# A two-layer hybrid decoder trunk on one core: the opening reads a transposed copy of x, and squares are summed on other engines

## The reference, cut to what matters

```python
def rmsnorm(x, gain):
    y = x * lax.rsqrt(jnp.mean(x * x, axis=-1, keepdims=True) + EPS)
    return y * gain
def swiglu(x, w_gate, w_up, w_down):
    return (jax.nn.silu(x @ w_gate) * (x @ w_up)) @ w_down
for l in range(DEPTH):                                  # 2
    x = x + 0.5 * swiglu(rmsnorm(x, ffn1_norm[l]), ...) # hidden width 2816
    x = x + token_mixing(rmsnorm(x, mix_norm[l]), ...)  # attentions A, B, C, gates, w_out
    x = x + 0.5 * swiglu(rmsnorm(x, ffn2_norm[l]), ...)
```

## Time and profile before

| | |
|---|---|
| median of three runs | 1139.65 us |
| profiled execution, its own time | 1140.59 us |
| its span, first to last instruction | 1138.8 us |
| PE busy | 1133.4 us (100%) |
| DVE busy | 770.4 us (68%) |
| ACT busy | 630.4 us (55%) |
| POOL busy | 70.3 us (6%) |
| chain that ended last | PE 98%, ACT 1%, DVE 1% |
| DMA, mean over the span | 182 GB/s; 326 and 318 GB/s in the first two of 40 slices |

### The profile page before, as it was taken

The page is one execution under the profiler, slowest core; times in us unless marked ns, Lnnn a source line. Parts: engine busy times, 40 slices in busy tenths (PEclk is TensorE's granted clock), DMA queues, the critical chain, the costliest instruction groups (busy, mean ns, idle before and its releaser), DMA issues.

```text
span 1138.8 us, 16092 instructions
## 1 busy us (share of the span) xinstructions
PE 1133.4 (100%) x5975; PEld 966.9 (85%) x5975; DVE 770.4 (68%) x1055; ACT 630.4 (55%) x941; POOL 70.3 (6%) x79
## 2 busy tenths in 40 slices
PE   9999999999999999999999999999999999999999
PEld 7888888888888888888888888888888888888887
DVE  5766666868768676655766856678676695766655
ACT  6644455666684564544564544466666745544542
POOL 3020000202000000000020200002110000000000
PEclk9999999999999999999999999999999999999999
DMA  9955554545544665556566555636445445655521
GB/s 326 318 175 196 187 196 134 185 144 190 148 148 150 220 222 189 190 178 219 173 166 228 185 185 186 204 98 216 148 156 178 176 156 186 222 185 201 194 87 37
DMA packets 138828, 207.34 MB, mean 182 GB/s; under 512 B 6898, under 2 KB 99876, under 8 KB 138756
## 3 DMA queue, kind: packets, MB, share of 16 engines
q1 hardware_dynamic: 137364, 205.02, 54.5%
q0 software_dynamic: 752, 0.79, 0.7%
q10 hardware_dynamic: 640, 0.55, 0.2%
HBM read 205.29 MB, written 1.05 MB: 181 GB/s over the span
## 4 chain that ended last, share of the span: by engine, by line
PE 98%; ACT 1%; DVE 1%; issue 0%; DVEq 0%; ACTq 0%; POOL 0%; POOLq 0%
PE bank L560 28%; PE bank L530 16%; PE bank L534 16%; PE bank L533 16%; PE bank L564 15%; PE bank L546 1%; PE bank L859 1%; PE bank L849 1%; PE bank L830 1%; ACT probs L1202 1%; PE bank L848 1%; PE bank L877 1%; PE bank L668 0%; PE bank L569 0%; ACT w_high L1016 0%
## 5 line engine op out<-in xcount | busy, mean ns | idle before, releaser
L1300 DVE TENSOR_TENSOR w_low<-raw,w_high 128x1024 fp32r<-128x1024 f32 x388 | 464.2, 1232 | 282.1 <-ACT w_high L1016 281.4
L1016 ACT ACTIVATE w_high<-raw 128x1024 fp32r<-128x1024 f32 x387 | 393.6, 1055 | 318.4 <-PE bank L564 173.5
L560 PE MATMUL bank<-xT,w_high 128*128 128x512 f32 x1388 | 331.6, 390 | 0.1
L560 PEld LDWEIGHTS bank<-xT,w_high 128*128 128x128 f32 x1388 | 257.0, 188 | 51.2 <-DVE xT L1318 0.2
L564 PEld LDWEIGHTS bank<-xT,w_low 128*128 128x128 f32 x1408 | 175.7, 191 | 3.6
L564 PE MATMUL bank<-xT,w_low 128*128 128x256 f32 x1408 | 178.6, 283 | 0.0
L530 PE MATMUL bank<-w_high,xT 128*128 128x512 f32 (+1 forms) x440 | 171.3, 389 | 0.0
L534 PE MATMUL bank<-w_low,xT 128*128 128x512 f32 (+1 forms) x440 | 168.1, 382 | 0.0
L533 PE MATMUL bank<-w_high,xT 128*128 128x512 f32 (+1 forms) x440 | 168.1, 382 | 0.0
L530 PE MATMUL bank<-w_high,oT_high 128*128 128x512 f32 x418 | 162.6, 389 | 0.0
L534 PE MATMUL bank<-w_low,oT_high 128*128 128x512 f32 x418 | 162.2, 388 | 0.0
(11 more groups left out here) (146 smaller groups left out, 770.8 us busy)
## 6 DMA issues: line engine op xcount, KB each, us to landing
raw<-in_w_in SPq DMA_DIRECT2D x92, 512.0 KB, 4.5
raw<-in_ffn_w_down SPq DMA_DIRECT2D x88, 512.0 KB, 4.2
raw<-in_ffn_w_gate SPq DMA_DIRECT2D x86, 512.0 KB, 4.0
raw<-in_ffn_w_up SPq DMA_DIRECT2D x86, 512.0 KB, 5.0
raw<-in_w_out SPq DMA_DIRECT2D x16, 512.0 KB, 4.4
raw<-in_w_branch_c SPq DMA_DIRECT2D x8, 512.0 KB, 3.9
raw<-in_w_branch_a SPq DMA_DIRECT2D x4, 512.0 KB, 4.0
raw<-in_w_branch_b SPq DMA_DIRECT2D x4, 512.0 KB, 5.9
```

What stands on the lines that cost most here:

```text
L560: return nc.tensor.matmul(bank[b0 + n][:, :], w_high[:, slot, column(k, n)], xT[:, k], start=k == 0, stop=full_last and k == KB - 1)
L1016: act.activation(w_high[:, slot], raw[:, in_slot, (p % 2) * 1024:(p % 2) * 1024 + 1024], ACT.Copy).then_inc(sem["high_ready"], 1)
L1300: dve.tensor_tensor(w_low[:, slot], raw[:, FILL_SLOT[p // 2], (p % 2) * 1024:(p % 2) * 1024 + 1024], w_high[:, slot].bitcast(F32), ALU.sub ...
```

## The change

1. The host gives the kernel a transposed copy of x (`x_turned`, 1024 by 256) and one array with all gains as columns. SP loads x_turned in five pieces (1, 1, 2, 2 and 2 blocks of 128 rows) into the space of `o_nat`, between the first weights; ACT's queue loads the gains. The first weights come by k block, and not by pair.
2. `cold_chunk` has no transposes. ACT and DVE make the high and low parts of xT from x_turned in SBUF (`cold_start`, `cold_pairs`). DVE rounds the first 512 columns of weights as well.
3. The squares are made by POOL: two multiplications and one addition of 1024 elements per partition, one addition of 512 and one of 256 (`sum_block_squares`). PE sums over the partitions with two matmuls of one column (`sum_squares`), ACT copies the result (`norm_sq`). The turn of the norm's row comes two groups of products later in PE's order than before, behind pair 4's narrow products.
4. The natural x is loaded later by POOL's queue, ahead of the rotary tables; the tables' own loads are issued after the second hidden tile. Gains need no transposes or copies.
5. TURNS_AT and CONTEXTS_AT of the first twin move from pairs 19 and 21 to 20 and 22, in both layers.

```diff
-TURNS_AT = (19, 27, 35, 42)
-CONTEXTS_AT = (21, 29, 37, 44)
+TURNS_AT = (20, 27, 35, 42)
+CONTEXTS_AT = (22, 29, 37, 44)
-WARM_FIRST, WARM_SECOND, WARM_THIRD = 6, 3, 6
+X_BLOCKS = ((0, 1), (1, 1), (2, 2), (4, 2), (6, 2))
+WARM = 11
...
+            load_x_turned(0)
+            load_x_turned(1)
+            first_rows(sp, 1, 1, half_landed[1], (1,))
+            load_x_turned(2)
+            first_rows(sp, 2, 2, fill_landed[FILL_SLOT[0]])
+            load_x_turned(3)
+            first_rows(sp, 4, 2, third_landed)
+            load_x_turned(4)
+            first_rows(sp, 6, 2, fill_landed[FILL_SLOT[1]])
...
+            def sum_block_squares():
+                for first, pieces in ((0, (0, 1, 2)), (D, (3, 4))):
+                    for piece in pieces:
+                        pool.wait_ge(x_turned_landed[piece], 16)
+                    v = x_turned[:, first:first + D]
+                    pool.tensor_tensor(x_squares[:, first:first + D], v, v, ALU.mult)
+                for width in (D, D // 2, D // 4):
+                    pool.drain()
+                    pool.tensor_tensor(x_squares[:, 0:width], x_squares[:, 0:width], x_squares[:, width:2 * width], ALU.add)
+                pool.drain().then_inc(block_squares_summed, 1)
...
+                pool.wait_ge(sem["hidden_ready"], value("hidden_ready", layer, 2))
...
+                if layer == 0:
+                    for half in range(HALVES):
+                        pool.dma_start(x[:, half], a["x"][0, half * P:half * P + P, :]).then_inc(x_loaded, 16)
...
-            def cold_row():
+            def sum_squares():
                 pe.wait_ge(sem["up_summed"], 1)
-                turn_row(0, 1, 4)
-                pe.wait_ge(rows_loaded, 16 * 3)
-                nc.tensor.transpose(bank[5][:, 0:GAIN_ROWS], gain_rows[0:GAIN_ROWS, :], ident[0:GAIN_ROWS, 0:GAIN_ROWS]).then_inc(gains_turned, 1)
+                pe.wait_ge(block_squares_summed, 1)
+                for half in range(HALVES):
+                    last = nc.tensor.matmul(bank[4][:, half:half + 1], x_squares[:, half * P:half * P + P], ones[:, 0:1].bitcast(F32),
+                                            start=True, stop=True)
...
+            def cold_pairs():
+                def block_low(kb):
+                    return dve.scalar_tensor_tensor(xT_low[:, kb, :], x_turned[:, kb * S:kb * S + S], gains_all[:, 0, G_FFN1 + kb:G_FFN1 + kb + 1],
+                                                    xT_high[:, kb, :].bitcast(F32), ALU.mult, ALU.subtract)
...
+                for p in range(1, 4):
+                    dve.wait_ge(sem["blocks_high"], p + 1)
+                    block_low(2 * p)
+                    block_low(2 * p + 1).then_inc(sem["blocks_low"], 1)
+                    low(0, p)
```

More of the change, by code:

```diff
@@ L114 @@
 }
[L117 removed]
+CREDIT = {"pair_used": RING, "low_ready": 2 * RING, "blocks_turned": -4}
 def ring_slots(items, mix_first, mix_items):
@@ L685, in cold_chunk @@
                     high_part(0, n, w_high, True)
+                pe.wait_ge(half_low, 1)
+                for n in range(4):
+                    high_part(0, n)
+                pe.wait_ge(block0_low, 1)
+                for n in range(4):
+                    low_part(0, n)
+                pe.wait_ge(sem["blocks_high"], 1)
                 pe.wait_ge(sem["high_ready"], value("high_ready", 0, 1))
@@ L688, in cold_chunk @@
                     high_part(1, n, w_high)
-                turn(1, 0, 1)
                 pe.wait_ge(sem["blocks_low"], 1)
-                for k in range(2):
-                    for n in range(4):
-                        low_part(k, n)
+                for n in range(4):
+                    low_part(1, n)
                 pe.wait_ge(sem["low_ready"], value("low_ready", 0, 1))
-                for k in range(2):
-                    for n in range(4):
-                        last = high_part(k, n)
+                for n in range(4):
+                    last = high_part(1, n)
                 last.then_inc(sem["pair_used"], 1)
@@ L1005, in high @@
                 in_slot = FILL_SLOT[n]
-                if layer == 0 and p in first_landed:
-                    act.wait_ge(first_landed[p], 32)
+                if layer == 0 and p == 0:
+                    act.wait_ge(half_landed[1], 32)
+                elif layer == 0 and p == 2:
+                    act.wait_ge(third_landed, 32)
                 else:
@@ L1357, in cold_first_chunk @@
                 low(0, p + 2)
+                low(0, p + 3)
                 dve.wait_ge(sem["row_ready"], 1)
@@ L1642, in _ @@
             dve.sem_inc(sem["low_ready"], CREDIT["low_ready"])
-            dve.wait_ge(first_gains_ready, 1)
-            dve.wait_ge(lam_init_ready, 1)
             for layer in range(DEPTH):
                 if layer == 0:
-                    for p in range(4):
-                        blocks_low(layer, ST_FFN1, p // 2, G_FFN1, (p % 2,))
-                        low(layer, p)
+                    cold_pairs()
                 else:
@@ L1680, in rotary_constants, with gain_columns @@
     return np.ascontiguousarray(table.reshape(2, HALVES, P, DH).transpose(2, 0, 1, 3).astype(np.float32))
+def gain_columns(inputs):
+    columns = [inputs[name].reshape(DEPTH, KB, P).transpose(2, 0, 1) for name in ("ffn1_norm", "mix_norm", "ffn2_norm")]
+    columns.append(inputs["diff_subln"].reshape(DEPTH, 1, P).transpose(2, 0, 1))
+    columns.append(np.broadcast_to(np.asarray(LAM_INIT, np.float32).reshape(1, DEPTH, 1), (P, DEPTH, 1)))
+    return np.ascontiguousarray(np.concatenate(columns, axis=2).astype(np.float32))
 def kernel(**inputs):
@@ L1688 @@
     arrays = {name: np.ascontiguousarray(inputs[name]) for name in _INS}
+    arrays["x_turned"] = np.ascontiguousarray(inputs["x"][0].T)
+    arrays["gains"] = gain_columns(inputs)
     arrays["trig"] = rotary_constants()
```

160 lines of the change are left out of this document (77 added, 83 removed).

## The result

The changed kernel takes 1143.17 us (median of 8 executions, 1142.69 to 1144.37), the kernel before 1140.0 (8 executions beside it, 1139.65 to 1140.31). The ratio is 1.0029, 95% interval 1.002 to 1.0038: slower, by 0.2 to 0.4%. The profiled execution has a span of 1140.9 us and took 1142.69.

The account below looks back on a forecast made before the run. PE was taken as the bound, busy 1133.4 of 1138.8 us. Opening +4.66 and twins -1.8 gave +2.86: 1143.45 from the profiled 1140.59, which lay 0.94 above the median, so 1142.5 as median; range 1136.0 to 1143.9.

Parts of the forecast that it names:

- turns by whole instructions: Opening: POOL and DVE alternate, one whole instruction each, on SBUF; first down product 4.66 us later; forecast's chance 0.42.
- the long DVE parts: Opening: DVE block and pair parts of 1.5 to 2.9 us beside POOL's squares, named as a sign of being right.
- an idle ahead of pair 1: Opening: PE idle 1.75 us before pair 1's products, which start at 10.85; named as a sign of being right.
- Start: Opening: first weights land at 5.0 us (4.6 to 5.6); PE's first product at 5.7 instead of 8.07, 2.4 us earlier.
- Pair 0: Opening: PE's 24 narrow products of pair 0 take 3.1 us, 0.3 more at the lower clock, and end at 9.1.
- POOL's durations: Squares in the opening: POOL takes 2.45 us for 1024 elements, 1.23 for 512, 0.61 for 256, in all 9.2 us.
- Rival 2: Opening: only subtractions of two SBUF tiles are held, block parts are not; +0.85 - 1.8, 1138.7 us; chance 0.15.
- Rival 1: Opening: only POOL is held up and DVE passes; down product at 31.2, 1.6 earlier; 1136.25 us; chance 0.26.
- Sum and row: Before the first down product: PE's sum 0.4 us, row's turn to hidden tile's low part 6.2, new PE idle 1.15.
- Twins: Second twin's transposes, each layer: turning one pair later removes a 0.9 us PE wait, -1.8 us in all.
- Sum: Whole kernel: opening 4.66 us later, less 1.8 for the twins' turn, gives +2.86 us.
- rival 3: Opening, pair 2: PE's 4.0 us idle also brings the lower clock back; +1.1, 1143.6 us; chance 0.13.

## Why the prediction was right, and where its steps were not

It named slower with 1142.5; 1143.17 was measured, within the range. The range, 1136.0 to 1143.9, took in rivals on both sides, so lying in it says little; the waits and the experiments say more. The mechanism was the one forecast: removing POOL's instructions is worth 5.4 us, and cutting them, moving them and adding them to the kernel before each moved the holds as turns by whole instructions would. That the number came so near is in part luck. From pair 0 to pair 3 PE was to wait 6.75 us (1.75, 4.0, 0.5 and 0.5) and waited 3.76 (0.94, 0.51, 1.23 and 1.08); the later start (0.65), pair 0 (0.45) and the products of pairs 1 to 3, slower by 0.8 in sum, took most of the difference back. Of the signs named ahead, the long DVE parts, the idle ahead of the down product and the turn without a wait came; an idle ahead of pair 1 did not, and the one ahead of pair 2 was small. Step by step:

- **Start** at 5.7: 6.35 measured, because the weights landed at 5.78; 5.0 was taken, 5.6 the latest. By the prediction's own words it would then fail as a whole; it did not, since the holds behind the start came all the same. In the other kernels with this same opening the first product began at 5.50 to 6.65, so it is a spread between executions, which one profile of before could not show.
- **Pair 0** to end at 9.1: it ended at 11.14. The step that failed let DVE finish the second k block's weights at 7.5, before POOL's first multiplication; ACT began its high part only at 7.45, when the weights had landed, POOL was first (7.85), and the half pair was held to 10.30. In the profile of the kernel with the row earlier DVE was first (7.50), POOL ended at 9.95 as predicted, and PE waited 1.36 us ahead of pair 1 (1.75): which of the two comes first differs between executions.
- **POOL's durations**: 1.89 and 2.08 for 1024 elements, 2.39 for the addition; 2.45 was taken, which is near for the addition and too long for the multiplications. That is the mis-sized term. By it DVE was at block 4 (12.15) before POOL could begin the second multiplication (12.30), so pair 2 waited 0.51 and not 4.0 us. POOL had waited 2.55 us for the last blocks of x there, whose landing was put at 11.5 and came at about 12.2. With 2.45 us for the first multiplication DVE's pair part would have ended at about 12.8, behind that landing, and POOL would have been first; this is worked out, not run. Both errors together: pairs 4 and 5 at 23.24 instead of 24.4.
- **Turns by whole instructions**: right, for the block parts too (2.11 and 1.51 us). Rival 2 held them free, and for block parts that read PSUM it would have been right, as the kernel before with POOL's work shows. The rule that the prediction cited from the "GPSIMD Engine Reference" of the Trainium skill (section "Key points"), two SBUF inputs, is thereby borne out on both sides. Rival 1, POOL gives way, holds for no row.
- **Sum and row**: 0.36 us for the sum (0.4), 6.26 from the row to the down product (6.2), an idle of 1.17 (1.15). All three terms were right. From 23.24 they give 36.41.
- **Twins** -1.8: right, by two experiments.
- **Sum**: +2.86 was +2.1 in the profiled executions (3.6, 0.4 more by the second chunk, less 1.9). The medians differ by 3.2, since the profile of before lay above its median, that of after below its own, and rival 3, the clock, which had 0.13 for itself, came true in most executions (0.999) at a price of 0.9 us, from the medians above. The long idle of 4.0 us for which it had been put is not in the profile; in the kernel with the row earlier it was behind short ones.

## What to carry to other kernels

Work given to an idle GpSimd is not free if VectorE works on two SBUF tiles at that time: each VectorE instruction can be late by what is left of the GpSimd instruction that runs, and GpSimd by VectorE's. Before moving a source from PSUM into SBUF, ask whether GpSimd works at that time: block parts from PSUM kept their 0.43 to 0.44 us beside it, those from SBUF took up to 2.11. Look for idle stretches on the engines that are waited for (ScalarE 1.94 us, VectorE 1.77 us here), put the work there, and then start the chain behind it a group earlier; that order turned +3.2 into -3.3 us (-1.5 without the twins' turn). A wait of TensorE is to be priced with the clock it may lose behind it.

## What the runs showed of the hardware that was not expected

- GpSimd multiplies 1024 elements of float32 with themselves in 1.89 us, about the time that 768 of two different inputs took (1.84).
- With two SBUF inputs each, VectorE and GpSimd alternate instruction by instruction: pieces of 256 elements held a VectorE pair part 0.4 us, but a GpSimd addition of 256 then took 1.4 us in the mean, where the one of 256 in the changed kernel took 0.73.
- The clock also fell without an idle: behind 3.5 us of float32 products of two columns the wide group took 3.01 us instead of 1.95, granted clock 0.66 in that stretch. Eight of ten executions had a lower mean clock. Why is not shown.
- The first weights land at a time that varies by 1.15 us between executions with the same queue in front of them: VectorE's rounding behind them began at 4.93 (POOL's work after the blocks) to 6.08 (squares summed by TensorE).
